# Half of a filter's frequencies on TensorE, folded squares on GpSimd, and a new start and end, in a float32 two-block model

## The reference

```python
def rmsnorm(x, g):
    y = xf * lax.rsqrt(jnp.mean(xf * xf, axis=-1, keepdims=True) + EPS)
    return (y * g.astype(jnp.float32)).astype(x.dtype)
...
    k = jnp.concatenate([fwd, jnp.zeros((1, HY_ORDER, D), f32), bwd[1:][::-1]], axis=0)
    return k / jnp.sum(jnp.abs(k), axis=0, keepdims=True)
...
    kf = jnp.fft.rfft(hyena_filters(L, fw1, fb1, fwi, fbi, fw3, freq), axis=0)
    for o, gate in enumerate((x1, x2)):
        z = gate.astype(f32) * (long_conv(z, kf[:, o]) + fbias[o].astype(f32) * z)
```

## Time and profile before

| | us |
|---|---|
| median of 3 runs | 3052.69 (3052.58 to 3054.29) |
| the profiled execution, its own time | 3051.69 |
| its span in the profile | 3049.9 |
| PE busy | 2972.4 (97%) |
| DVE busy | 2030.6 (67%) |
| ACT busy | 1632.7 (54%) |
| POOL busy | 249.4 (8%) |

### The profile page before, as it was taken

How to read it: one execution, slowest core, us unless ns; L and a number is a source line. 1 busy time by engine, 2 the same in 40 slices (tenths; PEclk the granted TensorE clock), 3 DMA queues, 4 the chain that set the end, 5 groups by cost and what they waited for, 6 DMA issues and landing times.

```text
span 3049.9 us, 46933 instructions
## 1 busy us (share of the span) xinstructions
PE 2972.4 (97%) x20370; PEld 2725.7 (89%) x20370; DVE 2030.6 (67%) x1817; ACT 1632.7 (54%) x1611; POOL 249.4 (8%) x199
## 2 busy tenths in 40 slices
PE   8999999999989999999999899999899999999999
PEld 7999999999978888888788497999799999786999
DVE  5787665688758888888788565554555455565553
ACT  5446444535557767767676462445644454353442
POOL 0130110023000000000000202100001010012010
PEclk9999999999989999999999899999999999999999
DMA  6444555544449989989899050556155555431453
GB/s 214 160 143 154 177 179 171 184 148 149 156 161 371 349 344 361 367 336 351 341 377 363 16 166 28 176 177 228 48 174 177 183 180 177 141 112 55 140 185 119
DMA packets 358819, 613.15 MB, mean 201 GB/s; under 512 B 11375, under 2 KB 323397, under 8 KB 323536
## 3 DMA queue, kind: packets, MB, share of 16 engines
q1 hardware_dynamic: 354592, 597.73, 56.3%
q10 hardware_dynamic: 3536, 12.23, 1.2%
q0 software_dynamic: 480, 0.12, 0.0%
HBM read 608.99 MB, written 1.05 MB: 200 GB/s over the span
## 4 chain that ended last, share of the span: by engine, by line
PE 94%; ACT 3%; DVE 2%; issue 1%; DMA 1%; ACTq 0%; POOLq 0%; POOL 0%; DVEq 0%
PE ps L327 18%; PE ps L329 18%; PE ps L328 18%; PE ps L1191 5%; PE ps L1193 5%; PE ps L1192 5%; PE ps L1172 3%; PE ps L1170 3%; PE ps L1171 3%; PE ps L1670 2%; PE ps L628 2%; PE ps L1685 2%; PE ps L1640 2%; PE ps L354 1%; PE ps L1626 1%; PE ps L1240 1%
## 5 line engine op out<-in xcount | busy, mean ns | idle before, releaser
L271 DVE TENSOR_TENSOR wlo<-raw,whi 128x2048 fp32r<-128x2048 f32 (+1 forms) x573 | 1314.0, 2299 | 609.2 <-ACT whi L260 605.2
L260 ACT ACTIVATE whi<-raw 128x2048 fp32r<-128x2048 f32 (+1 forms) x573 | 1083.7, 1894 | 276.3 <-PE ps L329 145.0
L327 PE MATMUL ps<-HX,whi 128*128 128x256 f32 x1808 | 519.2, 287 | 10.4 <-DVE wlo L271 5.6
L329 PE MATMUL ps<-HX,wlo 128*128 128x256 f32 x1808 | 513.4, 284 | 0.0
L328 PE MATMUL ps<-HX,whi 128*128 128x256 f32 x1808 | 513.3, 284 | 0.0
L327 PE MATMUL ps<-HXB,whi 128*128 128x256 f32 x1760 | 500.3, 284 | 0.0
L329 PE MATMUL ps<-HXB,wlo 128*128 128x256 f32 x1760 | 498.1, 283 | 0.0
L328 PE MATMUL ps<-HXB,whi 128*128 128x256 f32 x1760 | 498.1, 283 | 0.0
L327 PEld LDWEIGHTS ps<-HX,whi 128*128 128x128 f32 x1808 | 349.0, 193 | 13.6 <-ACT whi L260 6.1
L328 PEld LDWEIGHTS ps<-HX,whi 128*128 128x128 f32 x1808 | 349.0, 193 | 0.9 <-issue 0.5
L329 PEld LDWEIGHTS ps<-HX,wlo 128*128 128x128 f32 x1808 | 348.7, 193 | 0.0
(11 more groups left out here) (317 smaller groups left out, 4355.7 us busy)
## 6 DMA issues: line engine op xcount, KB each, us to landing
raw<-in_c_experts SPq DMA_DIRECT2D x264, 1024.0 KB, 4.9
raw<-in_w_in SPq DMA_DIRECT2D x72, 1024.0 KB, 5.0
raw<-in_ff_w_gate SPq DMA_DIRECT2D x44, 1024.0 KB, 5.3
raw<-in_ff_w_up SPq DMA_DIRECT2D x44, 1024.0 KB, 5.3
raw<-in_ff_w_down SPq DMA_DIRECT2D x32, 1024.0 KB, 5.1
raw<-in_dense_w SPq DMA_DIRECT2D x30, 1024.0 KB, 5.3
raw<-in_hy_w_in SPq DMA_DIRECT2D x24, 1024.0 KB, 5.1
raw<-in_ff_w_down SPq DMA_DIRECT2D x16, 768.0 KB, 4.7
```

The source lines that it names most:

```text
L260: e.activation(m.whi[:, i % NSPLIT, 0:n], m.raw[:, i % NRAW, 0:n], ACT.Copy).then_inc(*k.up("act", "hi", i))
L271: e.tensor_tensor(m.wlo[:, i % NRAW, 0:n], m.raw[:, i % NRAW, 0:n], hi, ALU.subtract).then_inc(*k.up("dve", "lo", i))
L327: e.matmul(o, wh, xh, start=first and t == k0, stop=False)
L329: i = e.matmul(o, wl, xh, start=False, stop=final and t == k1 - 1)
```

## The change

1. **Sums of squares.** `pe_sums` between gemms is gone. POOL folds the squares (`pool_sums`): 128x512 added onto 128x512 three times, then 128x256 onto 128x256. PE then does one ones-matmul, after the next stage's first gemm. For two norms (after the second HGRN mixer and before the second Hyena layer) POOL folds chunks 0 to 5 alone and PE does three matmuls. The two norms around the final norm of the first block keep their eight matmuls.
2. **Spectra.** The tokens lie with the even ones in one half and the odd ones in the other (filters, decay, the turned `z` by slices `j:L:2`, and the tables). For half the frequencies PE makes the even tokens' part and the odd tokens' part apart, one matmul each, so 8 instead of 16 matmuls for each filter; ACT evicts the odd part (4 of 128x512 instead of 8), and DVE adds and subtracts (8 more of 128x512, new `dve_spectra`), which gives both halves of the frequencies. `dve_spectra` of the first filter stands ahead of the preparation of `HX`, that of the second behind it.
3. **Start.** `X` comes in two DMAs, the first panel as two of 0.5 MB, the constants other than the vectors are issued by SP behind the first six panels, ACT's table is loaded ahead of the data, squares stand last, DVE's lower-bound work stands behind the first two feeds. PE starts with the chunks 0 to 3 (`pe_first`).
4. **End.** `X` is written in four DMAs (chunks 0-3, 4-5, 6, 7).

```diff
-def pe_last_sums(e, k, m, s):
-    pe_sums(e, k, m, s, 6, 2)
-    k.release("sum", s)
+def pe_last_sums(e, k, m, s, whole=True):
+    o = pe_take(e, k, m, "sum", s)
+    e.wait_ge(*k.at("sq sum", s))
+    i = e.matmul(o[:, 0:L], m.ones[:, :], m.sq[:, 0, :], start=True, stop=whole)
+    for c in () if whole else (6, 7):
+        e.wait_ge(*k.at("sq", s, c))
+        i = e.matmul(o[:, 0:L], m.ones[:, :], m.sq[:, c, :], start=False, stop=c == 7)
+    i.then_inc(*k.up("mm", "sums", s))
+def pool_sums(e, k, m, s, whole=True):
+    q = m.buf(11)
+    for c in (2, 4, 6) if whole else (2, 4):
+        e.wait_ge(*k.at("sq", s, c + 1))
+        e.tensor_tensor(q[:, 0:2 * L], q[:, 0:2 * L], q[:, c * L:(c + 2) * L], ALU.add).then_inc(*k.up("pool"))
+        e.wait_ge(*k.own("pool"))
+    e.tensor_tensor(q[:, 0:L], q[:, 0:L], q[:, L:2 * L], ALU.add).then_inc(*k.up("pool", "sq sum", s))
...
-    pe_hold(e, k, m, "sum", s)
-    pe_gemm(e, k, m, s, "out", m.HX, range(4), fresh=("mx", s),
-            after=lambda j: pe_sums(e, k, m, s, 2 * j - 2, 2) if j else None)
+    pe_gemm(e, k, m, s, "out", m.HX, range(4), fresh=("mx", s))
...
-                for fr in range(2):
-                    o = pe_take(e, k, m, "spec", s, o_, part, fr, c)
-                    for j in range(2):
-                        mm = e.matmul(o[:, :], dft[:, part, j, fr * 128:fr * 128 + 128],
-                                      src[:, j * 1024 + c * 512:j * 1024 + c * 512 + 512], start=j == 0, stop=j == 1)
+                for j in range(2):
+                    o = pe_take(e, k, m, "spec", s, o_, part, c, j)
+                    e.matmul(o[:, :], dft[:, part, j, 0:128], src[:, j * 1024 + c * 512:j * 1024 + c * 512 + 512],
+                             start=True, stop=True).then_inc(*k.up("mm", "spec", s, o_, part, c, j))
...
+def dve_spectra(e, k, m, s, o_):
+    for part in range(2):
+        for c in range(2):
+            lower, upper = spectrum_parts(m, o_, part, c)
+            e.wait_ge(*k.at("spec", s, o_, part, c, 0))
+            e.wait_ge(*k.at("free", "spec", s, o_, part, c, 1))
+            o = ps(k, m, "spec", s, o_, part, c, 0)[:, :]
+            e.tensor_tensor(lower, o, upper, ALU.add).then_inc(*k.up("dve"))
+            e.wait_ge(*k.own("dve"))
...
     dve_halves(e, k, m, s, last, 1)
+    dve_spectra(e, k, m, s, 0)
     dve_norm_alone(e, k, m, last, m.buf8(0), m.rs[:, :], gain)
-    for o_ in range(2):
-        e.wait_ge(*k.at("l1", s, o_))
-        e.reciprocal(scale_columns(m, o_), ps(k, m, "l1", s, o_)[:, 0:8]).then_inc(*k.up("dve", "free", "l1", s, o_))
+    dve_factors_l1(e, k, m, s, 0)
+    dve_spectra(e, k, m, s, 1)
+    dve_factors_l1(e, k, m, s, 1)
...
-    e.dma_start(out, m.X[:, :, :]).then_inc(*k.land("out_done", "out"))
+    for c0, c1 in ((0, 4), (4, 6), (6, 7), (7, 8)):
+        for c in range(c0, c1):
+            e.wait_ge(*k.at("x", last, c))
+        e.dma_start(out[:, c0:c1, :], m.X[:, c0:c1, :]).then_inc(*k.land("out_done", "out"))
```

More of the change, by code:

```diff
@@ L212, in panel_list @@
     hgrn(0)
+    first = a["w_in"][0][:, 1024:1280]
+    out[0:1] = [[(0, 4, 256, kview(first, 0, 256, 4 * h, 4 * h + 4))] for h in range(2)]
     ffn(a["dense_w1"][0], a["dense_w3"][0], a["dense_w2"][0])
@@ L490, in act_begin @@
         e.dma_start(m.qkg[half, 1:2], a["at_k_gain_2"].rearrange("o d -> d o")).then_inc(*k.land("consts_in", "consts"))
+def act_begin(e, k, m, a, panels):
+    e.dma_start(m.par[:, :], a["c_vectors"]).then_inc(*k.land("vectors_in", "vectors"))
+    e.wait_ge(*k.at("ones"))
+    e.activation(m.small[:, 40:41], m.epst[:, 0:1], ACT.Exp).then_inc(*k.up("act"))
     e.wait_ge(*k.at("vectors"))
-    for c in range(4):
-        act_ahead(e, k, m, "x", 2 * c, 2, (m.HX, lambda c: m.col("norm_mix", c)))
+    for half in range(2):
+        for c in range(4 * half, 4 * half + 4):
+            e.wait_ge(*k.at("x", "x", c))
+            e.activation(m.HX[:, 0, c, :], m.X[:, c, :], ACT.Copy, scale=m.col("norm_mix", c)).then_inc(*k.up("act", "xh", "x", c))
+        act_feed(e, k, m, panels)
     e0, e1 = m.small[:, 8:16], m.small[:, 16:24]
@@ L497, in act_begin @@
     e.activation(e1, e1, ACT.Exp).then_inc(*k.up("act", "lb exp"))
+    for c in range(4):
+        act_square(e, k, m, "x", 2 * c, 2)
 def pool_begin(e, k, m, a):
@@ L502, in pool_begin, with dve_begin @@
     e.memset(m.epst[:, :], EPS).then_inc(*k.up("pool", "ones"))
[L505 to L512, removed]
+def dve_begin(e, k, m, panels):
     lo = m.par[:, COLS["lower_bounds"]:COLS["lower_bounds"] + 16]
@@ L520, in dve_begin @@
     e.tensor_tensor(e1, l1, mx, ALU.subtract).then_inc(*k.up("dve", "lb less"))
+    for half in range(2):
+        dve_ahead(e, k, m, "x", 4 * half, 4, (m.HX, lambda c: m.col("norm_mix", c)))
+        dve_feed(e, k, m, panels)
     e.wait_ge(*k.at("lb exp"))
@@ L655, in act_hgrn @@
         act_panel(e, k, m, panels)
+        if l == 0 and j == 0:
+            act_panel(e, k, m, panels)
         if j == 0:
@@ L925, in pool_hgrn, with pe_ffn @@
             pool_times_norm(e, k, m, s, name, j, x, "normed", s, name, j)
-def pe_ffn(e, k, m, s, last, after=None, sums=True):
+def pe_ffn(e, k, m, s, last, after=None):
     for j in range(11):
@@ L952, in pe_ffn @@
             k.note("mm", "used", i)
-            if j and k0 == 0 and sums:
-                if j == 1:
-                    pe_hold(e, k, m, "sum", s)
-                pe_sums(e, k, m, s, 2 * j - 2, 2)
 def hidden_parts(m, j):
@@ L1705, in pe_hyena @@
     pe_back(e, k, m, s, 1, 1)
-    pe_hold(e, k, m, "sum", s)
-    pe_gemm(e, k, m, s, "out", m.HX, range(4), fresh=("zx", s),
-            after=lambda j: pe_sums(e, k, m, s, 2 * j - 2, 2) if j else None)
+    pe_gemm(e, k, m, s, "out", m.HX, range(4), fresh=("zx", s))
 def act_absolute(e, k, m, s, o_):
@@ L2060, in pe_attn @@
     back(3)
-    pe_hold(e, k, m, "sum", s)
-    pe_gemm(e, k, m, s, "out", m.HX, range(4), fresh=("ax", s),
-            after=lambda j: pe_sums(e, k, m, s, 2 * j - 2, 2) if j else None)
+    pe_gemm(e, k, m, s, "out", m.HX, range(4), fresh=("ax", s))
 def act_attn(e, k, m, a, panels, s, last, nxt):
```

102 lines of the change are left out of this document (67 added, 35 removed).

## The result

The changed kernel takes 3021.66 us (median of 4, 3014.77 to 3023.1) against 3053.49 us (median of 4 on the same chip): a ratio of 0.989, 95% interval 0.9873 to 0.9908. Forecast were 3020.4 us and 3005 to 3035.

The account below looks back on a forecast made before the run. PE was taken as the bound on most of the path, except the start, mixer-end rings and spectra. Norm sums 21.3, spectra 1.0, start 8.5 and end 1.5 made 32.3 us: 3052.7 - 32.3 = 3020.4 us, range 3005 to 3035.

Parts of the forecast that it names:

- The nets: Norms after feed-forward nets 0, 1, 2: seven matmuls of 0.435 us go at each, 3.0 us each, 9.1 in all.
- The rings: Mixer ends: the DVE-ACT loop of chunks and panels limits gains to 1.0 (first HGRN), 1.9 (attention), 2.3 per Hyena layer.
- Pooling: Norm after the pooling layer: two GpSimd folds between DVE's instructions lose 2.5 of 3.3 us, so 0.8 stays.
- The spectra: Hyena layers: GpSimd and DVE set the end; 1.3 us gained less 0.5 for the clock per layer, 1.0 taken together.
- within 2 us of its old distance from the halves: Sign for the Hyena layers: the first gemm after the spectra stays that near its old distance from the token halves.
- The start: Kernel start: the second gemm begins at 20.1 instead of 28.64 us, 8.5 us gained.
- The end: Kernel end: writing X in smaller last pieces gains 1.5 us, at most 2.6.
- (a): Rival, whole kernel: PE is the bound everywhere, all removed matmuls count, 70.4 us, 2982.3 us; chance 0.05.
- halfway case: Halfway to the rival that PE bounds everywhere: spectra give 6 us each and pooling 3.3, 3007 us; chance 0.17.
- (b): Rival: folds delay DVE feeds at seven mixer or net ends, 1.5 us each, spectra at low clock, 3036 us; chance 0.2.
- (c): Rival: slower than before, last folds come behind PE's first gemm at 11 norms, PE waits, 3084 us; chance 0.02.
- (d): Rival: PE's halves only become waits, spectra give 0 and start 5, 3025 us; counted within the main case.

Follow-up runs that it names:

- e3: The kernel before with only the folded sums of squares added (the input's norm, start, end and spectra as before): 3030.5 us, ratio 0.9923.
- e6: The changed kernel with ScalarE's squares moved behind its feed of the next panel at four mixer ends: 3014.6 us, ratio 0.987.
- e2: The changed kernel with the spectra made as before, 16 matmul pairs per filter and tokens in their old order: 3018.9 us, ratio 0.9889.
- e8: e7 with GpSimd adding up the second filter's absolute values only once VectorE has prepared HX: 3008.1 us, ratio 0.9851.
- e1: The changed kernel itself, run again without an edit: 3018.6 us, ratio 0.9884.
- e4: The kernel before with only the new start (including the input's folded squares) and the four-piece end added: 3044.2 us, ratio 0.9965.
- e12: The changed kernel itself, run once more without an edit in a later group: 3016.9 us, ratio 0.988.
- e5: The changed kernel with VectorE's eight small lower-bound operations moved behind the feeds of the third and fourth panels: 3018.0 us, ratio 0.9888.
- e7: The changed kernel with PE's spectra order turned, absolute sums later, and VectorE's first reciprocal within the preparation of HX: 3020.0 us, ratio 0.989.

## Why the prediction was right, point by point

The total lay 1.3 us from the number, and that closely it was luck. Executions of the changed kernel scatter over 8 us, and inside the sum a pooling stage and an end that gave more than forecast met a start that gave less in the first trace. What is no luck is that the large terms held one by one.

**The nets** gave 3.02 us each in every trace with folded sums, as 7 x 0.435 = 3.0 says. **The rings** were right in mechanism and size: 0.9 for 1.0, in the Hyena layers 2.05 for 2.3, in the attention layer 1.6 for 1.9 (the growth over its last gemms, the same in e3 and in the three traces). e6 showed that the ring was the bound. **Net 3 to the second Hyena** gave 2.1 for 2.2, the second HGRN mixer's end 2.1 to 2.8 for 1.7; why it gave more is open.

**Pooling** was mis-sized. I took 2.5 of 3.3 us as lost to folds and 0.8 as left. Net 2 and pooling gave 5.6 to 6.0, 4.8 in e3; less the net's 3.0 that is 1.7 to 3.0. The rows of the changed kernel:

```profile
2414.98 1.89 DVE L448 SCALAR_TENSOR_TENSOR HXB<-X,par,HXB 128x256 fp32r<-128x256 f32 x2
2417.36 1.20 DVE L2395 TENSOR_TENSOR X<-X,work 128x512 f32<-128x512 f32 x1
```

The same two groups take 0.87 and 0.69 us elsewhere in the stage, so two folds cost 1.02 + 0.51 = 1.5 us. The step that failed is the price of a fold to VectorE. I charged two whole folds of 1.25, but an instruction that comes in the midst of a fold waits for the rest of it only. At the same granted clock (0.79 over the stage's 16 us in before and in e3) the place gave 1.7, close to 3.3 - 1.5 = 1.8. In the three traces of the changed kernel the granted clock there is 0.89 to 0.97, and I put what is above 1.7 down to it; no run tests that.

**The spectra.** The path was the forecast one, wait for wait: PE idle ahead of the first sum until GpSimd is done (15.1 us behind the first spectrum matmul; forecast 14.7), a second idle ahead of the last spectrum matmul released by the reciprocal (0.91 us in the second layer, 0.12 in the first), VectorE's operations on PSUM in 7.1 us (2634.04 to 2641.10; forecast 7.1). The sum had `HX` 1.6 us too late: I added three GpSimd additions of 2.53 to sixteen instructions of 0.4, but the three that were shut out hold their own 0.4 within the 2.5, which is 1.2 of the 1.6 by which 14.0 is above 12.4. So the first gemm came 3.0 us nearer to the first spectrum matmul in the second layer, and not 1.3, and the sign "within 2 us of its old distance from the halves" missed: the distance fell from 26.0 to 23.0 us. The layers gave 2.5 to 2.8 and 0.0 to 3.0 in their gemms and the half clock took up to 1.5 of each again behind them, where I had 0.5 each; the median of e2 says 0.3 in all. So the 1.0 us that I took was near the truth by a balance of two terms that were both larger than I had them. Both readings lie inside the range I gave (-4 to +12). The Trainium skill, "SBUF — State Buffer", section "Who interferes with whom", gives the rule behind the 2.5 us: two SBUF inputs on VectorE and a reading GpSimd instruction exclude each other, one SBUF input does not. e8 agrees on the first half (5.07 to 0.87), and on the second the operations with a PSUM input, 0.69 us each beside GpSimd's additions.

**The start.** VectorE's third feed began at 17.89 us and the second gemm at 20.32; forecast were 17.8 and 20.1. The start gave 6.9 and not 8.5 in that trace, as 20 to 24 us ran at a granted clock of 0.57; in e1, e2, e4 and e12 it gave 8.1 to 8.5. **The end** gave 2.1 for 1.5: the last pieces of 128 KB land in 1.9 us, where the megabyte took 3.9.

```profile
out<-X SPq DMA_DIRECT2D x2, 128.0 KB, 1.9
```

**The rivals.** (a) fell as a whole with e2: the removed spectrum matmuls counted nothing. Its halfway case needed 6 us per layer. (b) fell in its size: the folds hit in the pooling stage, for 1.5 us, and single feeds by 0.3 (L273 of 2.56 to 2.58 instead of 2.29), not for 10. (c) had no place: no ones-matmul of a norm waited for a fold in the changed kernel; e5 made one wait for 1.62 us and e6 one for 0.68. (d) was half right: PE's halves did become waits, but the start gave 7 to 8.5 us and not 5.

## What to carry to other kernels

Work taken from the busiest engine is worth what the next wait behind it leaves. Write that chain out before halving anything, and plan the reordering together with the halving: here the halving alone gave nothing to be measured, and 24 us came once three waits were gone. Two of the three were not for data. One was GpSimd's additions set beside VectorE's two-input work, the other a PSUM bank whose reader stood behind other work. Removing one wait of a chain may only bring out the next (e7: 8 us gone, 6 us in its place), so a null result is no verdict on the idea before the trace is read.

## What the chip showed that was not expected

The lock works both ways. With VectorE's feeds in front, a fold of 128x256 took 2.65 us instead of 0.74 (e5), and in e6 ten of the folds of 128x512 took 2.8 to 2.9 instead of 1.3.

A weight load with a stride of two costs something. Those of the turning matmuls took a median of 209 ns in the changed kernel, 140 before, and 140 again in e2, where the tokens are contiguous. The line shows the lowest, the median and the highest:

```profile
L1699 PEld LDWEIGHTS ps<-ident,work x64: 194/209/231, 1804.4 to 2769.7; 128*128 128x128 f32 x64
```

The records then start 0.12 us apart and not 0.11, under 1 us in all, so taking nothing for it was right. The Trainium skill, "SBUF — State Buffer", section "Door 1: The DMA port swizzle", counts a stride up to four float32 as free; for these weight loads the measurement decides against it.

Executions of one program differ by up to 8 us (3014.8 to 3023.1 in twelve), and in the three traces most of the difference lies where TensorE's granted clock differs, so differences under 3 us had to be read from aligned traces, and even there stage by stage.
